# Index scores and the top-key search moved from attention into the projection

## The reference, cut to what matters

```python
h = layer_norm(concat([meta, x]), ln0_g, ln0_b)
proj = h @ w_in           # -> qa ka va | qb cb qi ki wi | gates (2 x 1024)
c_kv, k_idx = rms_norm(cb), layer_norm(ki)
# A: window attention with sinks, 8 heads of 64, window 128 + meta keys, ALiBi
# B: for each query over its visible keys
score = sum_h(w_idx[h] * relu(qi[h] . k_idx))      # 8 index heads
top   = top_k(score, 256)
logit = (q_b[h] w_uk[h]) . c_kv[top] / 8 - slope[h] * |position - top|
o     = softmax(logit) c_kv[top] w_uv[h]
h = layer_norm(a*h + (sigmoid(gA) * (A w_oa) + sigmoid(gB) * (B w_ob)) w_out)
out = layer_norm(a*h + (silu(h w_gate) * (h w_up)) w_down)
```

## Time and profile before

| | |
|---|---|
| median of 3 runs | 4190.16 us (4184.52 to 4199.81) |
| profiled execution, time and span | 4193.73 us, 4191.9 us |
| mean granted TensorE clock | 0.939 |
| PE busy | 3780.2 us (90%), 18641 matmuls |
| DVE, ACT, POOL busy | 1597.6, 1619.8, 1679.1 us |
| DMA | 346.65 MB, mean 83 GB/s |

### The profile page before, as it was taken

One profiled execution on the slowest core, in us unless ns is written; L12 is line 12 of the kernel. 1 busy time (PEld: TensorE's weight loads), 2 busy tenths in 40 slices (PEclk: granted clock), 3 DMA queues, 4 the chain that ended last, 5 costly groups with the idle time before them and its releaser, 6 DMA issues. The chain is left out here.

```text
span 4191.9 us, 52979 instructions
## 1 busy us (share of the span) xinstructions
PE 3780.2 (90%) x18641; PEld 3143.8 (75%) x18641; DVE 1597.6 (38%) x2415; ACT 1619.8 (39%) x2761; POOL 1679.1 (40%) x2019
## 2 busy tenths in 40 slices
PE   4999999948888898888997989799999999999997
PEld 3778788726667777777886777688878887887886
DVE  4211100045578888887532666311131031113102
ACT  2211111125577778878753222222222222222221
POOL 5211111035556555544202555444444444444443
PEclk9899999955689999999998999899999999999999
DMA  4322222120111100000004555333333333333332
GB/s 152 104 75 84 76 73 73 58 47 23 27 28 27 26 22 19 19 14 18 18 13 158 175 201 171 102 107 95 136 102 106 108 122 112 96 136 99 107 96 84
DMA packets 385538, 346.65 MB, mean 83 GB/s; under 512 B 20584, under 2 KB 329992, under 8 KB 383016
## 3 DMA queue, kind: packets, MB, share of 16 engines
q1 hardware_dynamic: 373808, 292.58, 23.3%
q10 hardware_dynamic: 11520, 51.38, 3.3%
HBM read 271.38 MB, written 72.52 MB: 82 GB/s over the span
## 5 line engine op out<-in xcount | busy, mean ns | idle before, releaser
L1699 POOL TENSOR_TENSOR ff_w_lo<-ff_raw,ff_w_hi 128x1024 fp32r<-128x1024 f32 x328 | 785.9, 2397 | 964.3 <-ACT ff_w_hi L1737 964.1
L1737 ACT ACTIVATE ff_w_hi<-ff_raw 128x1024 fp32r<-128x1024 f32 x328 | 346.0, 1056 | 860.6 <-PE ff_bank L98 743.0
L96 PE MATMUL ff_bank<-ff_h_hi,ff_w_lo 128*128 128x512 f32 x1408 | 551.1, 391 | 16.5 <-POOL ff_w_lo L1699 10.3
L98 PE MATMUL ff_bank<-ff_h_lo,ff_w_hi 128*128 128x512 f32 x1408 | 550.0, 391 | 0.0
L97 PE MATMUL ff_bank<-ff_h_hi,ff_w_hi 128*128 128x512 f32 x1408 | 549.9, 391 | 0.0
L1077 PE MATMUL at_ctx<-at_p_t,keys_c_nat 128*128 128x128 f32 (+1 forms) x2432 | 374.5, 295 | 36.0 <-ACT at_ctx_t L1234 35.4
L1077 PEld LDWEIGHTS at_ctx<-at_p_t,keys_c_nat 128*128 128x128 f32 (+1 forms) x2432 | 323.0, 201 | 76.3 <-ACT at_ctx_t L1234 53.0
L96 PE MATMUL ff_bank<-ff_w_hi,ff_f 128*128 128x512 f32 x960 | 374.2, 390 | 4.9 <-DVE ff_mixed L1984 4.3
L98 PE MATMUL ff_bank<-ff_w_lo,ff_f 128*128 128x512 f32 x960 | 373.6, 389 | 0.0
L97 PE MATMUL ff_bank<-ff_w_hi,ff_f 128*128 128x512 f32 x960 | 373.5, 389 | 0.0
L96 PE MATMUL in_acc<-pj_h_hi,in_w_lo 128*128 128x512 f32 x896 | 356.6, 398 | 5.8 <-POOL in_w_lo L439 5.8
(11 more groups left out here) (250 smaller groups left out, 6814.7 us busy)
## 6 DMA issues: line engine op xcount, KB each, us to landing
ff_raw<-in_w_ff_gate SPq DMA_DIRECT2D x88, 512.0 KB, 3.8
ff_raw<-in_w_ff_up SPq DMA_DIRECT2D x88, 512.0 KB, 3.8
ff_raw<-in_w_ff_down SPq DMA_DIRECT2D x88, 512.0 KB, 3.5
proj<-in_row SPq DMA_DIRECT2D x112, 256.0 KB, 2.0
pj_raw<-in_w_in SPq DMA_DIRECT2D x32, 512.0 KB, 4.6
ff_f<-proj SPq DMA_DIRECT2D x64, 256.0 KB, 3.5
ff_raw<-in_w_out SPq DMA_DIRECT2D x32, 512.0 KB, 3.4
keys_c_nat<-in_x SPq DMA_DIRECT2D x16, 512.0 KB, 4.1
```

Of the source, the lines that this page charges most:

```text
L96: pe.matmul(out, lhs_lo, rhs_hi, start=start, stop=False)
L98: return pe.matmul(out, lhs_hi, rhs_lo, start=False, stop=stop)
L1699: pool.tensor_tensor(w_lo[u][:, :], raw[u][:, :], f32(w_hi[u][:, :]), ALU.subtract).then_inc(lo_ready[u], 1)
L1737: act.activation(w_hi[u][:, :], raw[u][:, :], ACT.Copy).then_inc(hi_ready[u], 1)
```

## The change

`project` becomes `project_and_select`, and everything that leads to the masked distances leaves `attention`.

- The layer norm stage now makes the sums of eight chunks (`FIRST_CHUNKS`: the four key chunks and the index queries) behind the tiles, two behind each tile. `h_hi` and `h_lo` hold only two groups of 512 columns each; groups 0 and 1 are stored to DRAM (`h_kept`, 8 MB in all) and overwritten by groups 2 and 3.
- A new stage (scope `se`) projects the other 24 chunks as 96 units of 24 matmuls: first all chunks over groups 2 and 3, then, after groups 0 and 1 are loaded back, all chunks again over those (48 weight loads). A unit is cut into eight pieces of three matmuls, and `piece_steps` deals the pieces to 158 steps (n = -38 to 119), in proportion to an estimate of the columns that the other engines have in each step. By that function: 8 pieces a step in the first six steps, 0 or 1 in the 24 steps of tiles -4 to -2, 2 or 3 at tiles -1 and 0, rising to 8 at tile 7, none in the three last steps of tile 7, 8 in each step of tiles 8 to 12, 35 and then 21 in the last two tiles.
- In the same steps run index scores, search and selection, as before in their order, with two buffers `big_i` and three of `rel`, and blocks of at most 976 columns (two for most tiles, three for the last). ACT now judges rounds 9 to 29 of its own tile itself (`verdict`). POOL's `w_lo` is made in four quarters between judgements.
- The latent keys and the masked distances of all tiles are stored to DRAM and loaded by attention: 3 MB of keys at its start, one tile of distances a tile. `distances` and all of index, search and selection are gone from attention. `big_l` and `dist` become two buffers each.
- `mix_and_ffn` is untouched. Operations of search and selection have the same code unless shown.

```diff
-KEY_CHUNKS = [4, 5, 10, 15]
+FIRST_CHUNKS, KEY_CHUNKS = [4, 5, 10, 15, 11, 12, 13, 14], 4
...
+IDX_AHEAD = 4 * HEADS
+FIRST_STEP, LAST_STEP = -IDX_AHEAD - 6, STEPS - HEADS - 1
+RELOAD_STEPS = 3
+WIDEST, RELS = 976, 3
...
+def unit_order():
...
+    units = [(c, g, k) for k, c in enumerate(OTHERS) for g in (2, 3)]
+    return units + [(c, g, len(OTHERS) + k) for k, c in enumerate(OTHERS) for g in (0, 1)], 2 * OTHERS
...
+                    def load_group(g):
+                        sp.wait_ge(acc_ready, LAST_OF_GROUP[g + 2] + 1 + START)
+                        sp.dma_start(f32(flat(h_hi[g])), h_kept[g, 0]).then_inc(h_loaded[g], 16)
+                        sp.dma_start(f32(flat(h_lo[g])), h_kept[g, 1]).then_inc(h_loaded[g], 16)
...
+                        part_a(n, 0)
+                        low_parts(n - 3, [0])
+                        part_b(n, 0)
+                        low_parts(n - 3, [1])
+                        part_a(n, 1)
+                        low_parts(n - 3, [2])
+                        part_b(n, 1)
+                        low_parts(n - 3, [3])
...
+                        m = n + IDX_AHEAD + 2
+                        pieces = pieces_in(n)
+                        for b in range(index_blocks(m))[:1]:
+                            index(m, b)
+                        for u, c in pieces[:len(pieces) // 2]:
+                            piece(u, c)
+                        for b in range(index_blocks(m))[1:]:
+                            index(m, b)
+                        for u, c in pieces[len(pieces) // 2:]:
+                            piece(u, c)
...
+                        t, i = 2 * q + 1, r - len(EXPONENTS) - 1
+                        if i <= 0:
+                            act.wait_ge(cand_ready[1], (len(EXPONENTS) + 2) * (q - 1) + r + 1 + START)
+                        else:
+                            act.drain()
+                            act.activation(verdict[:, :], one(count, 1), ACT.Sign, bias=limit[:, :])
+                            act.drain()
+                            act.activation(one(cand, 1), verdict[:, :], ACT.Identity, scale=steps[:, 1, i:i + 1], bias=one(cand, 1))
+                            act.drain()
...
+                        part_b(n, 0)
+                        for b in range(index_blocks(m + 1))[:1]:
+                            rectify(m + 1, b)
+                        for u in units_in(n - 2):
+                            k = UNITS[u][2]
+                            evacuate(u)
+                            if 0 < u <= NK:
+                                high_keys(u - 1)
+                            if u == LAST_OF_LOAD[k] and k + 2 < len(LOADS):
+                                high_part(k + 2)
+                        part_b(n, 1)
+                        for b in range(index_blocks(m + 1))[1:]:
+                            rectify(m + 1, b)
...
-        big_i, big_l = s.ps("big_i", [P, 1024]), s.ps("big_l", [P, 1024])
+        big_l = [s.ps(f"big_l{u}", [P, 1024]) for u in range(2)]
```

More of the change, by code:

```diff
@@ new lines, in selected, with score_of, one, measured @@
+            def selected(n):
+                t, h = divmod(n, HEADS)
+                return (t + 1, h) if 0 < t < TILES - 1 else (None, None)
+            def score_of(t):
+                return score[t // 2 % 2][:, t % 2, 0:width(t)]
+            def one(tile, c):
+                return tile[:, c:c + 1]
+            def measured(n):
+                if n < HEADS:
+                    return {-15: 0, -10: 1}.get(n)
+                return n // HEADS + 1 if n % HEADS == 6 and n // HEADS + 1 < TILES else None
@@ new lines, in _, with low_part @@
+                    for e in range(MANTISSA):
+                        pool.memset(one(powers, e), 2.0 ** -(e + 1))
+                    pool.drain()
+                    def low_part(k, quarters=range(4)):
+                        for e in quarters:
+                            if e == 0:
+                                pool.wait_ge(hi_ready, k + 1 + START)
+                            of = slice(2 * e, 2 * e + 2)
+                            last = pool.tensor_tensor(w_lo[k % 2][:, of, :], raw[k % 2][:, of, :], f32(w_hi[k % 2][:, of, :]), ALU.subtract)
+                            if e == 3:
+                                last.then_inc(lo_ready, 1)
@@ new lines, in index @@
+                    def index(m, b):
+                        t, h = divmod(m, HEADS)
+                        i = idx_at[m, b]
+                        a0, wb = cuts(t)[b]
+                        if h == 0 and b == 0:
+                            pe.wait_ge(qi_lo, t + 1 + START)
+                            pe.wait_ge(key_lo, t + 2 + START)
+                        if i >= 2:
+                            pe.wait_ge(rel_ready, i - 1 + START)
+                        for a in range(0, wb, 512):
+                            n = min(512, wb - a)
+                            cols = slice(a0 + a, a0 + a + n)
+                            pe.matmul(big_i[i % 2][:, a:a + n], qi_2[t % 2][:, h, :], ki_hi[:, cols], start=True, stop=False)
+                            last = pe.matmul(big_i[i % 2][:, a:a + n], qi_2[t % 2][:, h, :], ki_lo[:, cols], start=False, stop=True)
+                        last.then_inc(idx_ready, 1)
@@ L1137, in _ @@
                         weigh(item)
-                    for b in range(1, index_blocks(m)):
-                        index(m, b)
                     for item in turned[1][2:]:
```

1220 lines of the change are left out of this document (640 added, 580 removed).

## The result

The changed kernel takes 4225.2 us (4219.97 to 4230.95, four runs), the kernel before 4192.7 on the same chip: 1.0078 times as long, 95% interval 1.0055 to 1.0102. The forecast was 4097, with 0.80 on faster and a range up to 4195. It is slower by 0.8%, and the whole interval lies above the 0.5% that the prediction gave as what a measurement here can tell from no change.

A forecast was written before the change was run, and what follows sets the result against it. Projection leaves DVE and ACT idle; attention loads DVE, ACT and PE, its late tiles bound by PE. 280 + 12 + 924 + 34 + 893 + 15 + 1941 = 4099 us span, less 2: 4097; range 3980 to 4195.

The forecast's parts named there:

- PE's 679 us as a floor: Middle stage: PE's 96 projection units, 548 us, and index columns, 131, set the least it can last.
- Nothing hides them: Layer norm stage: sixteen more sums of 24 matmuls add their full 91 us, ending the stage at 280.
- the middle stage's block limit: Middle stage, t = 0 to 14: each block lasts for its busiest engine, sum 748 us, with the factor 808.
- DVE the others: Middle stage: ACT sets blocks t = 0 to 4 and 13, DVE the other limits up to t = 14.
- The factor 1.08: Middle stage: measured over counted time, averaged on four earlier attention tiles, raises the limits from 748 to 808 us.
- The lead: Start of the middle stage: six units of 5.7 us and two waits of 4, 42 us.
- Two waits of 4 us: Start of the middle stage: two waits of 4 us, as weights are split three steps after they are freed.
- The start-up: Start of attention: 27.5 us left of 106.8, plus 0 to 15 for key latents ahead of queries; 34 taken.
- A: Middle stage: Sign and Sigmoid need different tables, two loads (2.57 us) a gate unit; 4232 us, chance 0.10.
- B: Middle stage: three engines at 85 to 95% catch each other, factor 1.18, +75 us, some 4172; chance 0.12.
- C: Middle stage and attention: coupling costs nothing (factor 1.02), second logit buffer brings 860; about 4019 us, chance 0.08.
- D: Projection and attention: PE bounds both stages, so the change does nothing; no chance of its own, in B's time.

The follow-up runs named there:

- e1: Changed kernel with two of the three products of every middle-stage projection piece left out, waits kept: 4206.0 us, stage 1026.
- e7: Changed kernel with one more [128 x 1] operation and a drain in every judgement of POOL: 4322.8 us, stage +103.
- e9: Changed kernel with each index sum replaced by one multiplication that reads one operand and writes its row sum: 4170.2 us, stage 995.
- e18: e16 with index scores rectified into SBUF and summed from there everywhere, index products two steps ahead: 4242.0 us, 1.0125 of the kernel before.
- e16: e11 up to step 24 and e13 behind it: 4178.7 us, 0.9974 of the kernel before.
- e4: Changed kernel with every tally of the bit search counting only the first 144 columns: 4098.9 us, stage 928.
- e12: Changed kernel with the index sum of e9 and the doubled first operation of each judgement of e7: 4245.4 us.
- e8: Changed kernel with POOL's weight splits cut to 8 columns of 128 a quarter, PE using the high part for the low: 4189.5 us, stage -31.
- e3: Changed kernel without POOL's inverse roots of the 17 key tiles and DVE's wait for them: 4221.9 us, stage 1043.
- e11: Changed kernel with the orders of e5 and e2 together for steps before -24 only: 4207.7 us, 1.0042 of the kernel before.
- e17: e16 with attention's first queries, distances and window loaded ahead of the latents' natural copy and second part: 4171.9 us, 0.9962 of the kernel before.
- e2: Changed kernel with POOL splitting the weights of a load two steps after it is freed, not three: 4233.5 us, 1.0107 of the kernel before.
- e5: Changed kernel with turned keys' copy (ACT) and low part (DVE) taken earlier, ahead of the next key tile's norm: 4226.3 us, 1.0096 of the kernel before.
- e13: Changed kernel rectifying in place, summing from PSUM, index products one step ahead, copies out earlier, all weights split two steps after freed: 4195.3 us, 1.0019 of before.

## Why the prediction was wrong

**What held.** Attention: 893 forecast, 902.5 measured, tiles 14 and 15 at 81.6 and 78.0, PE the bound as argued from the earlier trace rows. Switch 12 and 10; tail 15 and 11; the end 1941 and 1941; t = 12 to 14 142 and 134.8. PE's 679 us as a floor, not a bound, held too (e1).

**What missed to the good.** The layer norm stage, 280 forecast (275 to 292), took 261.5. "Nothing hides them" was wrong: PE's busy time grew by 86 us (131.8 to 218.0), the stage by 72, so 14 us of the new sums went into time in which PE had been idle, and a sum cost 5.4 us and not 5.7. Without these 18 us the kernel would have been slower still.

**The step that failed is the middle stage's block limit**: "DVE the others", times 1.08, with POOL's judging counted only where "nothing covers" it, at t = 12. Blocks t = 0 to 11 take 757 us where this gives 666, and 91 of the stage's 124 us too many lie there. The judging is hardly covered anywhere (e7: 103 of an added 126 us come out). Two causes were shown. First, DVE's index sum and POOL's judgement exclude each other, so a round costs DVE's sum and then the rest of the judgement: 53 us over t = 0 to 11 by e9, 30 over t = 3 to 10 by e18 against e16. Second, in even blocks POOL judges for both searches and splits weights between, in order. That this list is itself on the path is shown by e4's block of 54.1 us with DVE at 25.6 and by e12 against e9; how many us it costs was not measured. The first cause fits where the excess is late: over t = 3 to 11 the blocks are 46 us above the forecast, and e9 takes 45 off them. It doesn't fit early: t = 0 to 2 are 46 us above it too, of which e9 takes 8, e8 5 and e3 6. What keeps the rest of those 46 us, in the blocks where the forecast had ACT as the limit and didn't count POOL at all, stays open.

The factor 1.08 was fitted on attention blocks, where DVE's latent operations (L1468), which take one operand from PSUM, lay between the tallies of a step too. The trace of before has 61 of the 322 L902 start under a latent operation, and these keep their 0.36 us; 26 start under an index sum. In the changed kernel 83 of the 161 L706 start under an index sum. So part of the cover that the factor stood for was there before and went with the change; how many us of the factor it was is not shown.

The evidence was in the earlier trace rows. L902 is a [128 x 1] operation with a mean of 534 ns over 322; I took it as its price. The tile view of before has it as (ns, min, median, max)

```profile
L902 POOL TENSOR_SCALAR at_step<-at_count,at_wanted,at_steps x322: 363/364/3908, 914.7 to 2062.7; 128x1 f32<-128x1 f32 x161
```

so its price is 364. The 170 ns a time above it, 55 us in all, were nearly all time held: 47 of them lie in operations that started under one of DVE's sums, scans or scalings. The timelines of before, POOL's and DVE's, show one of these:

```profile
1544.52 2.84 POOL L902 TENSOR_SCALAR at_step<-at_count,at_wanted,at_steps 128x1 f32<-128x1 f32 x1 [0.97 <-DVE at_junk_v L1360]
```

```profile
1544.33 2.85 DVE L1388 TENSOR_TENSOR_SCAN at_score<-at_equal 128x1296 f32<-128x1296 bf16 x1
```

**The lead**, 42 forecast, was mis-sized by 27, and the four short blocks behind it (74) by 13. "Two waits of 4 us" were two kinds of wait in parallel: for the split, and for `low_keys`, which DVE's list places behind the norm that PE has just made possible (5.7 us at a time). e11 shows 15 of the 27. What keeps the rest stays open.

**The start-up**, 34 forecast, took 49.7. DVE's selection of the last tile ends 12 us behind PE's last product, which I had not counted; and the latents ahead of the first query load cost 7.8 us (e17 against e16), within the 0 to 15 given.

**Rivals.** A (two tables): false. The stage has one load, when Sigmoid first comes, and Sign, Relu, Identity and Copy ran on among the 64 Sigmoids:

```profile
L867 ACT ACT_TABLE_LOAD x1 | 1.3, 1283 | 0.0
```

By the Trainium skill (ScalarE: Activation LUTs, "Table sets: the hidden batching unit") cheap functions are in every set; the trace agrees, and for Sign beside Sigmoid too. B (engines catch each other) named the right stage and the right direction, with +75 for a measured +124, and the wrong reason: its "three engines at 85 to 95%" left out the fourth, POOL, which is busy for 56 to 66% of the blocks shown and whose short judgements stand between two tallies. Its sign, a block t = 11 of 88 us or more, did not come: t = 11 took 79.0 where 81 were forecast, and the excess grows towards the early blocks. C is out by the time, D by e1.

ACT's own judging of the odd tile (22 of 31 rounds, 8 to 29 counted from 0), estimated at 0.87 us a round, is 0.29 + 0.39 us of operations and 0.16 of gaps ahead of them in the trace, and was right. It keeps 154 of the odd tile's 217 judgements off POOL.

## What to carry to other kernels

Before work is counted as covered by another engine's, look in the trace at one operation of each that overlap: if the short one ends just behind the long one, the cover is none, and a tiny operation whose mean duration is well above its own fastest is the sign of it. In a schedule where each engine keeps its own order, an edit that removes one wait may show nothing until the wait beside it is gone too (e2 and e5 alone gave 0 and 6 us of the lead, together 15; e2's edit gave 65 in e13): test them in pairs before dropping them. And a factor fitted on one stage carries over only with what hid the small waits there.

## What the runs showed of the hardware

A POOL operation that starts while DVE sums two SBUF operands (L1008), scales float32 in SBUF (L1041, L1051) or scans (L1057) ends 0.05 to 0.27 us after DVE's operation, in each of 205 such cases of judging (L684 to L714) in the middle stage; one that starts under a tally, which writes its row sum, keeps its own duration (L712: 0.19 us, 126 times). It holds the other way round too: a sum of 336 columns, 0.56 us alone, that starts under POOL's split of index queries:

```profile
462.82 2.70 DVE L1008 SCALAR_TENSOR_TENSOR se_score<-se_rel,se_w_idx,se_score 128x336 f32<-128x336 f32 x1
```

```profile
462.79 2.37 POOL L658 TENSOR_TENSOR se_qi<-se_qi 64x1024 fp32r<-64x1024 f32 x1 [0.21 <-issue]
```

With one operand from PSUM the same sum held nothing (e13: L706 under it keeps 0.37 to 0.39 us, 79 times). The Trainium skill (SBUF — State Buffer, "Who interferes with whom") states this rule: a DVE instruction with two SBUF inputs and a GpSimd instruction that reads SBUF, or a DVE instruction in a two-port mode and a GpSimd instruction, exclude each other for the whole instruction, and the one that starts second waits. The trace agrees in these 205 cases; under the scaling of a first head (L1006), one L709 that started 24 ns behind it kept its own 0.19 us. It should have been a rival of the prediction, with the earlier trace rows as its evidence.

A smaller one: with two thirds of PE's products gone its mean granted clock over the stage fell from 0.87 to 0.65, and the stage didn't lengthen.
